# Product-key routing on one core: the first top-16 level moved into the score loop, and gate columns compared in one wide instruction and scaled on ScalarE

## The reference, cut to what matters

```python
q = (xt @ wq).reshape(t, PEER_HEADS, 2, PEER_HALF)
sc = jnp.einsum('thcd,hcnd->thcn', q, keys)          # 1024 tokens x 16 x 128 scores
v1, i1 = lax.top_k(sc[:, :, 0], PEER_TOPK)           # first level: 16 of 128, values and indices
v2, i2 = lax.top_k(sc[:, :, 1], PEER_TOPK)
cand = (v1[..., :, None] + v2[..., None, :]).reshape(t, PEER_HEADS, 256)
best, ci = lax.top_k(cand, PEER_TOPK)                # second level: 16 of 256
e = i1[ci // 16] * N_KEYS + i2[ci % 16]
g = jax.nn.softmax(best, axis=-1)
out = (gelu(x . u[e]) * g) . v[e]                    # per token, over 8 x 16 experts
```

## Time and profile before

| | us |
|---|---|
| median of three runs (lowest to highest) | 3452.57 (3450.69 to 3453.32) |
| the profiled execution, its own time | 3452.24 |
| its span | 3450.1 |
| `route`, the 32 scored items: first copy of scores to last | 824.6 to 1015.9 |
| `hidden`: first matmul to last gate matmul | 1027.2 to 2332.9 |
| of it, the 96 slots with gates | 1296.4 to 2332.9 |
| `weigh`: first matmul to last | 2370.2 to 3433.2 |

### The profile page before, as it was taken

One profiled execution on the slowest core, in us unless ns is written; L12 is line 12 of the kernel. 1 busy time (PEld: TensorE's weight loads), 2 busy tenths in 40 slices (PEclk: granted clock), 3 DMA queues, 4 the chain that ended last, 5 costly groups with the idle time before them and its releaser, 6 DMA issues. The chain is left out here.

```text
span 3450.1 us, 45082 instructions
## 1 busy us (share of the span) xinstructions
PE 3190.7 (92%) x17090; PEld 2873.6 (83%) x17090; DVE 2307.2 (67%) x4358; ACT 995.5 (29%) x1127; POOL 1662.2 (48%) x847
## 2 busy tenths in 40 slices
PE   7988678988989999999999999994999999999998
PEld 5776578877879999999999999993788888888886
DVE  2510678822118789999899999883676666666665
ACT  3211347722112223333333333331122212112110
POOL 2510010022203564555454545664878777777773
PEclk9999789999999999999999999997999999999999
DMA  3242552141224676676666666888887787787784
GB/s 131 89 167 83 144 107 47 29 165 67 92 62 138 212 235 205 226 249 232 240 233 236 229 243 233 288 314 317 303 311 281 286 303 273 288 305 275 288 295 154
DMA packets 262430, 722.32 MB, mean 209 GB/s; under 512 B 22000, under 2 KB 88432, under 8 KB 255088
## 3 DMA queue, kind: packets, MB, share of 16 engines
q1 hardware_dynamic: 188528, 451.52, 38.6%
q0 software_dynamic: 73728, 268.47, 22.1%
HBM read 581.50 MB, written 138.41 MB: 209 GB/s over the span
## 5 line engine op out<-in xcount | busy, mean ns | idle before, releaser
L1188 PE MATMUL hid_ps<-side_hi,u_hi 128*128 128x384 f32 x2048 | 533.1, 341 | 23.5 <-POOL u_lo L874 16.9
L883 POOL DMA_INDIRECT found<-in_u,pick_u x232 | 333.3, 1437 | 420.1 <-DVE found L1119 386.8
L1188 PE MATMUL hid_ps<-side_lo,u_hi 128*128 128x384 f32 x2048 | 524.1, 337 | 0.0
L1188 PE MATMUL hid_ps<-side_hi,u_lo 128*128 128x384 f32 x2048 | 523.8, 336 | 0.0
L1920 PE MATMUL part<-v_hi,act_hi 128*128 128x512 f32 x1536 | 476.4, 392 | 48.5 <-POOL act_lo L1843 48.3
L1920 PE MATMUL part<-v_lo,act_hi 128*128 128x512 f32 x1536 | 475.4, 391 | 0.0
L1920 PE MATMUL part<-v_hi,act_lo 128*128 128x512 f32 x1536 | 474.9, 391 | 0.0
L874 POOL TENSOR_TENSOR u_lo<-u_raw,u_hi 128x1024 fp32r<-128x1024 f32 x128 | 330.3, 2580 | 267.9 <-ACT u_hi L833 267.3
L1859 DVE TENSOR_TENSOR acc<-acc,part 128x1024 f32<-128x1024 f32 x192 | 234.4, 1221 | 319.8 <-PE part L1920 319.6
L1188 PEld LDWEIGHTS hid_ps<-side_hi,u_hi 128*128 128x128 f32 x2048 | 368.0, 190 | 24.2 <-issue 12.7
L1838 POOL TENSOR_TENSOR v_lo<-v_raw,v_hi 128x2048 fp32r<-128x2048 f32 x64 | 295.8, 4621 | 183.8 <-ACT v_hi L1811 183.2
(11 more groups left out here) (204 smaller groups left out, 5148.3 us busy)
## 6 DMA issues: line engine op xcount, KB each, us to landing
u_raw<-in_uT SPq DMA_DIRECT2D x128, 512.0 KB, 3.6
v_raw<-in_v SPq DMA_DIRECT2D x64, 1024.0 KB, 6.9
hid_d<-hid SPq DMA_DIRECT2D x128, 384.0 KB, 3.4
gate_d<-stage SPq DMA_DIRECT2D x48, 1024.0 KB, 6.1
act_in<-hid_d SPq DMA_DIRECT2D x64, 768.0 KB, 6.6
gate_in<-gate_d SPq DMA_DIRECT2D x32, 1536.0 KB, 14.5
w_raw<-in_w_in SPq DMA_DIRECT2D x6, 2048.0 KB, 8.3
k_hi<-k_hi_d SPq DMA_DIRECT2D x32, 256.0 KB, 8.1
```

What stands on the lines that cost most here:

```text
L883: pool.indirect_dma_start(found[:, g], None, u_d, bass.IndirectOffsetOnAxis(ap=pick_u[:, g, n:n + 1], axis=0))\
L1188: mm = pe.matmul(hid_ps[:, s % 2, half, 0:W], w[:, s % 2, ch], x[:, ch, GB * P + half * W:GB * P + (half + 1) * W], start=n == 0, stop=n = ...
```

## The change

Two things are changed.

First, the first level of the ranking moves from `hidden` to `route`. DVE no longer copies a score item out; it ranks its four streams where they lie in PSUM, and SP stores the 16 values and 16 indices of each stream (`top_d`, `top_ix_d`; two DMAs an item, rows of 64 bytes) in place of the 128 scores (one DMA, rows of 512 bytes). `hidden` loads those (`load_tops`) and starts its ranking with the sums; its steps are spread anew over the slots, and ACT's exponents with them.

Second, `gate_factors` makes `row_hot` and `col_gate` by one comparison of 128 x 1024 each, and ACT multiplies the gate value into `col_gate` with eight copies with a scale (`scale_columns`). PE waits for ACT's, not DVE's.

```diff
@@ route, SP @@
-                sp.wait_ge(sc_sb, n + 1)
-                sp.dma_start(score_d[4 * half:4 * half + 4, :, key * NK:(key + 1) * NK]
-                             .rearrange("b t n -> t b n"), sc[:, n % 2]).then_inc(sc_out[n % 2], 16)
+                sp.wait_ge(top_ok, n + 1)
+                for out_d, kept in ((top_d, top), (top_ix_d, top_ix)):
+                    sp.dma_start(out_d[4 * half:4 * half + 4, :, key * K:(key + 1) * K]
+                                 .rearrange("b t n -> t b n"), kept[:, n % 2]).then_inc(top_out[n % 2], 16)
@@ route, DVE @@
-            for n in range(SCORED):
-                dve.wait_ge(sc_ok, n + 1)
+            def reached(semaphore, value, step):
+                dve.wait_ge(semaphore, value)
+                dve.memset(tick[:, step:step + 1], 0.0)
+            def first_values(n):
                 if n >= 2:
-                    dve.wait_ge(sc_out[n % 2], 16 * (n // 2))
-                dve.tensor_copy(sc[:, n % 2], sc_ps[:, n % 2]).then_inc(sc_sb, 1)
+                    dve.wait_ge(top_out[n % 2], 32 * (n // 2))
+                reached(sc_ok, n + 1, 0)
+                for b in range(4):
+                    last = dve.max(top[:, n % 2, b, 0:8], sc_ps[:, n % 2, b])
+                last.then_inc(first_ok, 1)
+            def first_indices(n):
+                reached(first_ok, n + 1, 1)
+                for b in range(4):
+                    dve.max_index(top_ix[:, n % 2, b, 0:8], top[:, n % 2, b, 0:8], sc_ps[:, n % 2, b])
+                for b in range(4):
+                    last = dve.match_replace(rest[:, n % 2, b], top[:, n % 2, b, 0:8], sc_ps[:, n % 2, b], LOW)
+                last.then_inc(rest_ok, 1)
+            def second_values(n):
...
+            def second_indices(n):
+                reached(second_ok, n + 1, 3)
+                for b in range(4):
+                    last = dve.max_index(top_ix[:, n % 2, b, 8:16], top[:, n % 2, b, 8:16], rest[:, n % 2, b])
+                last.then_inc(top_ok, 1)
+            for n in range(SCORED + 1):
+                if n < SCORED:
+                    first_values(n)
+                if n >= 1:
+                    second_values(n - 1)
+                if n < SCORED:
+                    first_indices(n)
+                if n >= 1:
+                    second_indices(n - 1)
@@ route, PE, score_item @@
-                    pe.wait_ge(sc_sb, n - 1)
+                    pe.wait_ge(rest_ok, n - 1)
@@ hidden, ACT @@
+            def scale_columns(j, s):
+                act.wait_ge(hot_ok, j - NO_GATES + 1)
+                for i in range(TOK):
+                    t = s * TOK + i
+                    last = act.activation(col_gate[:, s % 2, i], col_gate[:, s % 2, i], ACT.Copy,
+                                          scale=g_t[:, t:t + 1])
+                last.then_inc(col_ok, 1)
...
-                    if phase == 0 and s == 6:
+                    if phase == 0 and s == 2:
                         exponents(0)
-                    if s == (14 if phase == 0 else 12) and not last:
+                    if s == (12 if phase == 0 else 9) and not last:
                         exponents(tb + 1)
+                    if phase >= GB:
+                        scale_columns(j, s)
@@ hidden, DVE, gate_factors @@
-                for b in range(2):
-                    t0 = s * TOK + BATCH * b
-                    dve.tensor_tensor(row_hot[:, s % 2, BATCH * b:BATCH * (b + 1)],
...
-                for i in range(TOK):
-                    t = s * TOK + i
-                    last = dve.tensor_scalar(col_gate[:, s % 2, i], iota[:, :], col_t[:, t:t + 1], g_t[:, t:t + 1],
-                                             ALU.is_equal, ALU.mult)
-                last.then_inc(col_ok, 1)
+                for hot, picked in ((row_hot, row_t), (col_gate, col_t)):
+                    last = dve.tensor_tensor(hot[:, s % 2],
+                                             iota[:, :].unsqueeze(1).to_broadcast([P, TOK, NK]),
...
+                last.then_inc(hot_ok, 1)
@@ hidden, DVE, rank @@
                 if s == 0:
-                    keys_first_values(tb)
+                    pair_sums(tb)
                 if s == 1:
-                    keys_first_indices(tb)
-                if s == 2:
-                    keys_take_out(tb)
+                    pairs_first_values(tb)
...
-                if s == 5:
-                    pair_sums(tb)
```

More of the change, by code:

```diff
@@ L386, in _, with route @@
                         last.then_inc(qt_ok, 1)
-def route(nc, a_hi, a_lo, x_first, ident, x_d, w_out_d, norm_g_d, wq_d, keysT_d, h_d, score_d):
+def route(nc, a_hi, a_lo, x_first, ident, x_d, w_out_d, norm_g_d, wq_d, keysT_d, h_d, top_d, top_ix_d):
     G = 6
@@ L445, in route @@
         sc_ok = sem("sc_ok")
-        sc_sb = sem("sc_sb")
-        sc_out = [sem("sc_out0"), sem("sc_out1")]
+        first_ok = sem("first_ok3")
+        rest_ok = sem("rest_ok3")
+        second_ok = sem("second_ok3")
+        top_ok = sem("top_ok3")
+        top_out = [sem("top_out0"), sem("top_out1")]
         block = c.enter_context(nc.Block())
@@ L663, in _, with hidden @@
                     score_item(n - 1)
-def hidden(nc, x_hi, x_lo, x_first, iota, iota16, ident, uT_d, u_d, score_d, hid_d, gate_d, pick_v, pick_act,
+def hidden(nc, x_hi, x_lo, x_first, iota, iota16, ident, uT_d, u_d, top_d, top_ix_d, hid_d, gate_d, pick_v, pick_act,
            blocks=TB):
@@ L767, in load_u, with load_tops @@
                     .then_inc(u_in, 16)
[L769 to L772, removed]
+            def load_tops(tb):
+                for kept, in_d in ((top, top_d), (top_ix, top_ix_d)):
+                    sp.dma_start(kept[:, :, :, :].rearrange("p h c k -> p (h c) k"),
+                                 in_d[bass.ds(tb, 1)].rearrange("o t (n k) -> t (o n) k", k=K)).then_inc(top_in, 16)
             def store_gates(tb, s, n):
@@ L915, in _ @@
         def _(dve):
-            streams = [(h, half) for h in range(H) for half in range(2)]
             def gate_factors(tb, s, early):
@@ L939, in reached @@
                 dve.memset(tick[:, :], 0.0)
[L943 to L964, removed]
-                    last = dve.max(top[:, h, half, 8:16], score[:, 2 * h + half])
-                last.then_inc(ranked, 1)
-            def keys_second_indices(tb):
-                reached(ranked, RANKS * tb + 4)
-                for h, half in streams:
-                    last = dve.max_index(top_ix[:, h, half, 8:16], top[:, h, half, 8:16], score[:, 2 * h + half])
-                last.then_inc(ranked, 1)
             def pair_sums(tb):
-                reached(ranked, RANKS * tb + 5)
+                dve.wait_ge(top_in, 32 * (tb + 1))
                 dve.tensor_copy(top_ixf[:, :, :, :], top_ix[:, :, :, :])
@@ L996, in pairs_take_out @@
             def pairs_take_out(tb):
-                reached(ranked, RANKS * tb + 8)
+                reached(ranked, RANKS * tb + 3)
                 for h in range(H):
@@ L1002, in pairs_second @@
             def pairs_second(tb):
-                reached(ranked, RANKS * tb + 9)
+                reached(ranked, RANKS * tb + 4)
                 for h in range(H):
@@ L1954, in layer @@
     h_d = dram("h_d", [T, D])
-    score_d = dram("score_d", [TB, P, 2 * PEER_HEADS * NK])
+    top_d = dram("top_d", [TB, P, 2 * PEER_HEADS * K])
+    top_ix_d = nc.dram_tensor("top_ix_d", [TB, P, 2 * PEER_HEADS * K], U32, kind="Internal").ap()
     hid_d = dram("hid_d", [NK, P, TD])
@@ L1977, in layer @@
             x_first = sb("x_first", [P, GB, D])
-            route(nc, side_hi, side_lo, x_first, ident, x, w_out, norm2_g, wq, keysT, h_d, score_d)
-            hidden(nc, side_hi, side_lo, x_first, iota, iota[:, 0:K], ident, uT, u, score_d, hid_d, gate_d,
+            route(nc, side_hi, side_lo, x_first, ident, x, w_out, norm2_g, wq, keysT, h_d, top_d, top_ix_d)
+            hidden(nc, side_hi, side_lo, x_first, iota, iota[:, 0:K], ident, uT, u, top_d, top_ix_d, hid_d, gate_d,
                    pick_v, pick_act)
```

66 lines of the change are left out of this document (35 added, 31 removed).

## The result

The changed kernel takes 3462.62 us (median of eight runs, 3456.64 to 3465.09); the kernel before, on the same chips, 3450.20 (3445.57 to 3453.32). The ratio is 1.0033, 95% interval 1.0023 to 1.0042: slower by 12.4 us, clear of noise. The prediction was +26.5 us (3478.7, range 3447 to 3512, slower 0.85). The direction and both places are as it says, and so is the store that each turn of DVE waits for; PE was held differently from what it says, and the size is off by a factor of two.

A forecast was written before the change was run, and what follows sets the result against it. The prediction took PE to bound the kernel, busy 3190.7 of 3450.1 us. To 3452.24 it added +67 in `route`, -40 in the gated slots and -0.5 at the start of `hidden`: 3478.7 us, range 3447 to 3512.

The forecast's parts named there:

- What bounds the kernel: Whole kernel: PE bounds it; in the gated slots DVE's lateness costs about 45 us, 27.3 of it visible waiting.
- Gain of 40 in the gated part: Gated slots of `hidden`: PE's waits for DVE go, except in the last block; -40 us, bounds 25 to 45.
- ACT's scaling: Gated slots: ACT's eight scaled copies take at most 2.5 us and fit into its 5.49 us idle before the Gelu.
- DVE's own work, 5.0 us: `route`: ranking one item's four streams takes DVE 5.0 us, below PE's 6.35, so work alone would not slow PE.
- The landing in each turn: `route`: each DVE turn adds a whole store, landing 2.3 us after issue; 7.77 us a turn against PE's 6.35.
- Who waits for the slow turn: `route`: PE waits for DVE before the score matmuls, some 1.4 us an item.
- Weight loads, 12 us: `route`: later weight loads hold ACT near items 10 and 18; 5.1 us each plus 1 each for PE's slow start.
- Route in all: `route` as a whole, ending near 1085.8 instead of 1018.9: +67 us; +58 with landings of 2.0, +100 with 3.5.
- Start of `hidden`, -0.5: From the end of `route` to the first matmul of `hidden`: 256 KB loaded in place of 1 MB, -0.5 us.
- The store is no bound: Rival, `route`: the store lands early enough that items keep 6.35 us; +27 there, 3439 us in all; chance 10%.
- Small rows land late: Rival, `route`: stores of 64-byte rows take 3.5 us to land, turn 8.97 us; 3511 us in all; chance 10%.
- The gates stay late: Rival, gated slots: holds behind POOL and in-order ACT keep PE waiting; gain 10 instead of 40, 3509 us; chance 12%.

The follow-up runs named there:

- gates_only: The kernel before with only the wide gate comparisons and the scaling on ACT, the first ranking level staying in `hidden`: 3442.0 us, ratio 0.9969.
- old_slots: The changed kernel with the remaining ranking steps, and ACT's exponents with them, put back into their slots of before the change: 3480.0 us, ratio 1.0077.
- the third slot: The changed kernel with three output slots in place of two for the kept values and indices in `route`: 3437.0 us, ratio 0.9958.

## Why the prediction was right or wrong, point by point

- **What bounds the kernel.** Right: 45 us of PE's time in the gated slots hung on DVE, and 46.0 went. That it cost more than the 27.3 us of visible waits is also right.
- **Gain of 40 in the gated part.** The term was 6 too small. Of its 45 us the prediction kept 3 for the last block and 2 more without a reason; both went. The reason given for the gain was partly wrong, and that the term is near is in part luck: it gave the wide comparisons 13 us a block and counted on the average load, 83%. `gates_only` (17% spare, 7.5 us gained) and `old_slots` show that the longest slots decide, and that the spread, which had no term, did half the work.
- **ACT's scaling.** 2.44 us a slot were taken at 2.5, and it fits, as the earlier trace rows let expect. The agreement is partly luck: one copy takes 0.39 us and not the 0.31 of the row, and they start every 0.3 us.
- **DVE's own work, 5.0 us.** 4.9.
- **The landing in each turn.** That DVE's turn is its work plus one whole store is right, and confirmed by removing the wait and by making it larger. The size of this term is the step that failed: I took 2.3 us from the store of 512 rows of 512 bytes; with rows of 64 bytes DVE goes on 1.93 us after the issue, landing and wake-up together. With 0.1 less of work the turn is 7.26, not 7.77, and 30 turns make 15 us. The Trainium skill (DMA: Bandwidth & Descriptors, Anatomy of one DMA) gives 2.0 us plus the bytes at 436 GB/s, fitted on the gpsimd path; its 2.1 us for 32 KB is an estimate, and these stores, which SP issues, take 1.9 in the trace. It was nearer than the row I chose. An eighth of the data did matter, and I had said that the row count decides.
- **Who waits for the slow turn.** Wrong, though it had no price of its own in the sum: the prediction had PE wait some 1.4 us an item for DVE. PE ran ahead at 6.35 us an item and waited for DVE once, 6.1 us before the last product. DVE's chain has the same length either way; but its lag is why a stand of 14 us on PE costs the stage only 6.3.
- **Weight loads, 12 us.** Foretold to the engine and the item, 5.1 each plus 2; the stands cost 6.3 and 6.2, the slow products behind them 1.6. The other 4.4 of the 18.5 are stores that landed late, for which there was no term; they differ by execution. In the profiled one the term was too small by 6.5, in the three others with this stage by 1.4 to 3.5.
- **Route in all.** +67 foretold; from the first score product to the landing of the last store it is 253.0 - 195.5 = +57.5.
- **Start of `hidden`, -0.5.** Wrong sign: from that landing to the first matmul 9.5 us, 8.3 before, +1.2. I costed the smaller load and not the operation that now stood beside POOL's first subtraction.
- **The sum.** 57.5 + 1.2 - 46.0 = 12.7 of the 13.0 us of span. Against +26.5, the turn and the gated part account for the difference of 13.8 with 15.3 + 5.9 and the tail with 0.6, the weight loads and the start of `hidden` for 6.5 + 1.7 the other way. The inner forecast of 3463 to 3497 does not follow from the stated bounds: with the nearer ones, +58 or +67 in `route` and -45 or -25 in the gated part, they give 3464.7 to 3493.7. The measured 3462.6 is below the lower end of either.
- **The rivals.** *The store is no bound* fell, and its price was right: made so by the third slot, the stage ends 30 us after that of before (foretold 27), and the time is 3437 (foretold 3439). *Small rows land late* fell. The Trainium skill (DMA: Bandwidth & Descriptors, Specifications) says that under 512 bytes the DMA engine reads, modifies and writes; a store of 512 such rows lands in 1.9 us here, below the 2.3 of 512-byte rows. *The gates stay late* fell for the changed kernel. Its small gain is that of `gates_only`, 7.5 us in the gated part, but for another reason: there the wide `row_hot` comparison takes 1.37 us in the mean, not 2.4, and the double table steps make PE wait.

The error is one of sums with opposite signs: +67 and -40 leave 27, and 14% of one term and 15% of the other made it half.

## What to carry to other kernels

A ring of two slots whose next user waits for a store gives no overlap if the store is issued at the very end of the turn before: ask not how many slots there are but what lies between the issue and the wait. When work is added to one engine's turn, look at what other queues issue behind its last step; here a weight load moved 17 us back (issued at 887.20, before at 870.12) and stopped three engines. Look also at who falls behind: with two slots between them PE ran ahead of DVE, and no wait of PE named DVE until the last item, though DVE set the length of the stage. When an engine is late only in some slots, its average load says little: take the step out of the longest slot, or spread the steps, before making every slot a little shorter.

## What the runs showed of the hardware that I had not expected

- A store of 32 KB in 512 rows of 64 bytes landed in 1.8 to 1.9 us in the median, one of 256 KB in 512 rows of 512 bytes in 2.3. A few of either landed late, after up to 3.9 and 4.9 us. In the kernel before such a landing cost nothing; in the changed one DVE's next turn starts later by it.
- SP's issue of the second of two such stores takes 0.51 us, the first 0.37.
- Two 128 x 512 comparisons and eight 128 x 128 ones cost DVE 4.9 us a slot with holds; two of 128 x 1024 cost 2.45, and the holds moved on to the dot products (1317 to 1743 ns).
- A two-tensor sum of 2048 columns on DVE (2.28 us) stretched a subtraction of 1024 on POOL from 2.34 to 4.20 us; beside DVE's `max_index` one took 2.38. The other way round, DVE's 128 x 512 comparison took 0.68 us in the mean without a subtraction of POOL beside it and 1.90 with one; `max`, `max_index` and `match_replace` of 128 columns took 0.27 to 0.29 either way.
- Eight scaled copies of 128 columns on ACT start every 0.3 us (2.44 for the eight).
